# Final norm of an encoder block: load the residual before the last two expert blocks are added, and redo their rows afterwards

## What is computed

```python
x = x + _hier_moe(_rmsnorm(x, norm_ffn_g), ...)   # each token: 2 of 32 experts
return _rmsnorm(x, norm_final_g)

# in _hier_moe: the (token, expert) pairs are sorted by expert, each expert's list is
# padded to whole blocks of 128 rows, and each block gives
a = silu(xblk @ w1[e]) * (xblk @ w3[e])
yb = a @ w2[e]                                     # scaled by the gate, added to the token's row
```

## Time and profile before

| | us |
|---|---|
| median of 3 runs | 2211.6 |
| lowest, highest | 2208.79, 2212.04 |
| profiled execution, device time | 2216.69 |
| its span in the trace | 2214.9 |
| mean granted TensorE clock | 0.952 of full |

### The profile page before, as it was taken

The page is one execution under the profiler, slowest core; times in us unless marked ns, Lnnn a source line. Parts: engine busy times, 40 slices in busy tenths (PEclk is TensorE's granted clock), DMA queues, the critical chain, the costliest instruction groups (busy, mean ns, idle before and its releaser), DMA issues. The chain is left out here.

```text
span 2214.9 us, 29378 instructions
## 1 busy us (share of the span) xinstructions
PE 1995.7 (90%) x8823; PEld 1404.3 (63%) x8824; DVE 1212.4 (55%) x1133; ACT 1063.1 (48%) x1283; POOL 817.7 (37%) x526
## 2 busy tenths in 40 slices
PE   3999999999999977979999389999898999999980
PEld 2436778777666322327777268888686888888870
DVE  6653223234667734744444655566767666665644
ACT  6871222226556332433333244555757556555634
POOL 0690000000000320322222055576867866675750
PEclk9999999999999998989999679999999999999995
DMA  6691222321234987957443358788989987887848
GB/s 218 238 327 39 76 67 76 95 76 41 50 79 137 348 310 301 347 196 238 169 152 105 143 171 277 218 307 291 370 287 371 376 286 249 306 291 224 304 132 322
DMA packets 206334, 476.88 MB, mean 215 GB/s; under 512 B 23569, under 2 KB 86165, under 8 KB 201111
## 3 DMA queue, kind: packets, MB, share of 16 engines
q1 hardware_dynamic: 165080, 383.61, 47.3%
q0 software_dynamic: 17824, 58.79, 11.6%
q10 hardware_dynamic: 23360, 33.56, 4.8%
HBM read 355.25 MB, written 114.29 MB: 212 GB/s over the span
## 5 line engine op out<-in xcount | busy, mean ns | idle before, releaser
L1921 PE MATMUL p<-wh_hi,x_hi 128*128 128x512 f32 x768 | 313.2, 408 | 22.2 <-DVE wh_lo L2048 14.2
L1867 POOL DMA_INDIRECT xg<-scratch_H,curidx x196 | 285.3, 1456 | 89.8 <-issue 44.8
L1921 PE MATMUL p<-wh_lo,x_hi 128*128 128x512 f32 x768 | 307.7, 401 | 0.0
L1921 PE MATMUL p<-wh_hi,x_lo 128*128 128x512 f32 x768 | 307.4, 400 | 0.0
L2048 DVE TENSOR_TENSOR wh_lo<-w_raw,wh_hi 128x2048 fp32r<-128x2048 f32 x128 | 284.7, 2285 | 26.1 <-ACT wh_hi L1996 26.1
L540 PE MATMUL ps<-h_hi,wp_hi 128*128 128x512 f32 x640 | 257.6, 403 | 4.3 <-DVE wp_lo L735 4.3
L540 PE MATMUL ps<-h_lo,wp_hi 128*128 128x512 f32 x640 | 254.3, 397 | 0.0
L540 PE MATMUL ps<-h_hi,wp_lo 128*128 128x512 f32 x640 | 254.3, 397 | 0.0
L1996 ACT ACTIVATE wh_hi<-w_raw 128x2048 fp32r<-128x2048 f32 x128 | 234.0, 1903 | 0.0
L1886 POOL TENSOR_TENSOR wy_lo<-w_raw,wy_hi 128x2048 fp32r<-128x2048 f32 x32 | 187.7, 5865 | 90.8 <-ACT wy_hi L1999 90.5
L1921 PEld LDWEIGHTS p<-wh_hi,x_hi 128*128 128x128 f32 x768 | 147.0, 191 | 59.1 <-DVE wh_lo L2048 15.8
(11 more groups left out here) (329 smaller groups left out, 3588.8 us busy)
## 6 DMA issues: line engine op xcount, KB each, us to landing
w_raw<-in_exp_w_dram SPq DMA_DIRECT2D x384, 512.0 KB, 7.5
dec<-in_decay_dram SPq DMA_DIRECT2D x32, 512.0 KB, 5.5
scratch_KA<-work SPq DMA_DIRECT2D x32, 512.0 KB, 4.5
scratch_SI<-arena SPq DMA_DIRECT2D x32, 512.0 KB, 4.5
kin<-scratch_KA SPq DMA_DIRECT2D x21, 512.0 KB, 7.5
arena<-scratch_SA SPq DMA_DIRECT2D x21, 512.0 KB, 6.0
wp_raw<-in_w_in_dram SPq DMA_DIRECT2D x18, 512.0 KB, 3.8
h_raw<-in_x_dram ACTq DMA_DIRECT2D x4, 2048.0 KB, 15.3
```

The costliest lines, as they stand in the source:

```text
L1867: pool.indirect_dma_start(out=xg[:, j, :], out_offset=None, in_=quarter_rows, in_offset=bass.IndirectOffsetOnAxis(ap=cur[:, j:j + 1], axis ...
L1921: mm = pe.matmul(acc[:, :], x[:, k, :], w, start=(k == 0 and i == 0), stop=(k == n - 1 and i == 2))
```

## The change

Four things change. (1) POOL no longer adds the two last blocks before it lets SP start: it raises `mostly_added` when the loop's last scatter has landed and PE has used the last first-layer weights. (2) `final_norm` treats all 16 tiles as before. POOL waits for the 16 loads, then scatters the two last results one after the other, gathers the rows of these two blocks (128 each) from `X2`, waits for all 32 stores, and scatters the two normed tiles over `out`, waiting for the first before it issues the second. ACT and DVE norm them as tiles 16 and 17. The row lists come from `spot`: `late_row` is `spot` cut at 2047, so every empty row becomes row 2047, and `late_out` its place in `out`. Four small DVE operations in `route` make them. (3) The second late result has a buffer of its own, `yb_last`, and ACT stores it when it has come to tile 5. (4) For the last expert, the sixth weight split moves from POOL to DVE.

The core of the diff:

```diff
 # route, vector
+            dve.wait_ge(idx_set, BASE + 2)
+            step(dve.tensor_scalar(late_row[:, :], spot[:, :], SEQ - 1, None, ALU.min))
+            step(dve.tensor_scalar(late_out[:, :], late_row[:, :], HALF - 1, 5, ALU.bitwise_and, ALU.logical_shift_left))
+            step(dve.tensor_scalar(late_tile[:, :], late_row[:, :], 6, None, ALU.arith_shift_right))
+            dve.tensor_tensor(late_out[:, :], late_out[:, :], late_tile[:, :], ALU.add).then_inc(weight_set, 1)
 # experts, gpsimd
             def split_last(e, B, r):
+                if e is LAST:
+                    return
...
             B = per_block(pool, "pool", body, split_last)
-            for last in range(2):
-                scatter(B + last)
-                added(B + last)
-            pool.sem_inc(all_added, 1)
+            pool.wait_ge(used, BASE + B * KC)
+            pool.sem_inc(mostly_added, 1)
             pool.wait_ge(xg_in, B * 64 + 128)
             pool.sem_inc(pool_passed, 1)
+            pool.wait_ge(marks["weight_set"], BASE + 2)
+            for last in range(2):
+                for i, rows_of in enumerate((late_row, late_out, spot)):
+                    pool.tensor_copy(cur_late[:, last, i:i + 1], rows_of[:, ds(B + last, 1)]).then_inc(late_ready, 1)
+            for t in range(NT):
+                pool.wait_ge(marks["x_in"][t], 16)
+            pool.wait_ge(late_ready, BASE + 6)
+            for last, y in enumerate((yb, yb_last)):
+                pool.wait_ge(y_evac, BASE + B + last + 1)
...
+                pool.indirect_dma_start(out=rows, out_offset=bass.IndirectOffsetOnAxis(ap=cur_late[:, last, 2:3], axis=0),
+                                        in_=y[:, :], in_offset=None, compute_op=ALU.add).then_inc(y_out, 16)
+                pool.wait_ge(y_out, B * 16 + 16 * last + 16)
...
+            for last in range(2):
+                pool.indirect_dma_start(out=marks["x_late"][:, last, :], out_offset=None, in_=token_rows,
+                                        in_offset=bass.IndirectOffsetOnAxis(ap=cur_late[:, last, 0:1], axis=0)).then_inc(late_in[last], 16)
+            pool.wait_ge(marks["o_out"], 32 * NT)
+            for last in range(2):
+                pool.wait_ge(marks["late_normed"], last + 1)
+                pool.indirect_dma_start(out=dram["out"].rearrange("o t d -> (o t) d"), out_offset=bass.IndirectOffsetOnAxis(ap=cur_late[:, last, 1:2], axis=0),
+                                        in_=marks["x_late"][:, last, :], in_offset=None).then_inc(late_stored, 16)
+                pool.wait_ge(late_stored, 16 * last + 16)
 # experts, scalar
-            for last in range(2):
-                store_y(B + last)
-            act.sem_inc(act_passed, 1)
+            store_y(B)
+            marks["store_last"] = lambda: store_y(B + 1, yb_last)
 # experts, vector
             def split_w(e, B, r, some=range(D_PAIRS)):
-                for pair in some:
+                for pair in (range(PAIRS) if e is LAST else some):
 # final_norm, sync
-            sp.wait_ge(marks["all_added"], 1)
+            sp.wait_ge(marks["mostly_added"], 1)
 # final_norm, scalar
-            for t in range(NT):
-                if t + 1 < NT:
+            for t in range(NT + 2):
+                if t == STORE:
+                    marks["store_last"]()
+                if t + 1 < NT + 2 and t + 1 != NT:
                     square(t + 1)
                 act.wait_ge(inverse, t + 1)
                 act.activation(st[:, t, 3:4], st[:, t, 2:3], ACT.Sqrt).then_inc(root, 1)
+                if t + 1 == NT:
+                    square(NT)
 # final_norm, vector
-            for t in range(NT):
-                if t + 1 < NT:
+            for t in range(NT + 2):
+                if t + 1 < NT + 2 and t + 1 != NT:
                     invert(t + 1)
                 dve.wait_ge(root, t + 1)
...
+                dve.scalar_tensor_tensor(out=tile(t), in0=tile(t), scalar=st[:, t, 3:4], in1=gain[:, :],
+                                         op0=ALU.mult, op1=ALU.mult).then_inc(o_ready if t < NT else late_normed, 1)
```

More of the change, by code:

```diff
@@ L1582, in route @@
         marks.update(idx_set=idx_set, weight_mm=weight_mm, weight_set=weight_set)
-        LG, weight, idx, spot, nblk, tables = yield sem
+        LG, weight, idx, spot, nblk, tables, late_row, late_out = yield sem
         cursor = dict(wy=marks["wy_at"], xg=marks["xg_at"])
@@ L1610, in route @@
         ex, one1 = sb("ex", [P, NT]), sb("one1", [P, NT])
+        late_tile = put("wy", "late_tile", [P, IDX_COLS], I32)
         assert cursor["wy"] <= marks["wy_end"] and cursor["xg"] <= marks["xg_end"]
@@ L1771, in experts @@
         pool_passed, act_passed = sem("pool_passed"), sem("act_passed")
-        xg_in, y_out, all_added = sem("xg_in", 0), sem("ye_out", 0), sem("all_added", 0)
-        marks["all_added"] = all_added
+        xg_in, y_out, mostly_added = sem("xg_in", 0), sem("ye_out", 0), sem("mostly_added", 0)
+        marks["mostly_added"] = mostly_added
         rounded, lowered, lowered_last, used = sem("w_rnd"), sem("w_low"), sem("w_low_last"), sem("w_used")
-        D_PAIRS = PAIRS - 1
+        D_PAIRS, LAST = PAIRS - 1, N_EXP - 1
         spot_ready, y_added = sem("spot_ready"), sem("y_added")
+        late_ready, late_in, late_stored = sem("late_ready"), [sem(f"late_in{i}", 0) for i in range(2)], sem("late_stored", 0)
+        marks["late_in"] = late_in
         idx_ready, trx, xhi_ready, xlo_ready = sem("idx_ready"), sem("trx"), sem("xhi_ready"), sem("xlo_ready")
@@ L1779, in experts @@
             sem(n) for n in ("s_ready", "a_ready", "tra", "ahi_ready", "alo_ready", "y_done", "y_evac"))
-        nblk, idx, spot, weight, xT = yield sem
+        nblk, idx, spot, weight, xT, late_row, late_out = yield sem
         marks["raw_at"] = -(-nc.sbuf_base // 32) * 32
@@ L1790, in experts @@
         cur, cur_spot = sb("curidx", [P, 4], I32), sb("curspot", [P, 1], I32)
+        cur_late = sb("curlate", [P, 2, 3], I32)
         marks["xg_at"] = nc.sbuf_base
         xg = sb("xg", [P, 4, D // 4])
+        x_hi_at = -(-nc.sbuf_base // 32) * 32
         x_hi, x_lo = sb("x_hi", [P, KC, P], F32R), sb("x_lo", [P, KC, P], F32R)
@@ L1825, in per_block @@
                 blocks_of(N_EXP - 2, 0)
-                following(N_EXP - 1, eng.snap(B), 1)
+                following(LAST, eng.snap(B), 1)
                 blocks_of(N_EXP - 1, 1)
@@ L1978, in split_a, with store_y @@
                 act.activation(a_hi[:, :, :], pta.rearrange("p (k n) -> p k n", k=FT), ACT.Copy).then_inc(ahi_ready, 1)
-            def store_y(B):
+            def store_y(B, out=yb):
                 act.wait_ge(y_done, BASE + B + 1)
-                act.wait_ge(y_added, BASE + B)
+                if out is yb:
+                    act.wait_ge(y_added, BASE + B)
+                else:
+                    act.wait_ge(xlo_ready, BASE + B * 2)
                 for c in range(2):
-                    copy = act.activation(yb[:, c * 512:(c + 1) * 512], py[c][:, :], ACT.Copy, scale=weight[:, ds(B, 1)])
+                    copy = act.activation(out[:, c * 512:(c + 1) * 512], py[c][:, :], ACT.Copy, scale=weight[:, ds(B, 1)])
                 copy.then_inc(y_evac, 1)
@@ L2004, in _ @@
             split_w(0, 0, 0, range(H_PAIRS, PAIRS))
-            act.wait_ge(marks["weight_set"], BASE + 1)
+            act.wait_ge(marks["weight_set"], BASE + 2)
             act.wait_ge(a_ready, BASE + 1)
@@ L2050, in split_w @@
                         hi, lo = (v[:, r * FT + j - KC:r * FT + j - KC + 2, :] for v in wy)
-                        dve.tensor_tensor(lo, raw[:, j:j + 2, :], hi.bitcast(F32), ALU.subtract).then_inc(lowered, 1)
+                        dve.tensor_tensor(lo, raw[:, j:j + 2, :], hi.bitcast(F32), ALU.subtract).then_inc(lowered if pair < D_PAIRS else lowered_last, 1)
             dve.memset(a[:, :], 0.0).then_inc(a_ready, 1)
@@ L2078, in final_norm @@
         x_in = [sem(f"x8_in{t}", 0) for t in range(NT)]
-        squared, mean, inverse, root, o_ready = (sem(n, 0) for n in ("f_squared", "f_mean", "f_inverse", "f_root", "f_out"))
+        squared, mean, inverse, root, o_ready, late_normed = (sem(n, 0) for n in ("f_squared", "f_mean", "f_inverse", "f_root", "f_out", "late_normed"))
+        marks.update(x_in=x_in, o_out=o_out, late_normed=late_normed)
         yield sem
@@ L2082, in final_norm @@
         x, junk = at("xfin", [P, NT, D], marks["wh_at"]), at("junk8", [P, 2, D], marks["raw_at"])
-        gain, st = at("gain_fin", [P, D], marks["raw_at"] + 8 * D), at("st8", [P, NT, 4], marks["raw_at"] + 12 * D)
+        gain, st = at("gain_fin", [P, D], marks["raw_at"] + 8 * D), at("st8", [P, NT + 2, 4], marks["raw_at"] + 12 * D)
+        marks["x_late"] = x_late = at("x_late", [P, 2, D], marks["raw_at"] + 16 * D)
+        tile = lambda t: x[:, t, :] if t < NT else x_late[:, t - NT, :]
         out_t = dram["out"].rearrange("o (n l g) d -> l g n (o d)", g=2, l=NT)
+        STORE = 5
         block = yield
@@ L2102, in square @@
```

(23 more changed lines are left out.)

5 lines of the change are left out of this document (4 added, 1 removed).

## The result

| | before | changed |
|---|---|---|
| median of 5 runs, us | 2211.6 | 2221.6 |
| lowest, highest | 2208.79, 2215.10 | 2218.57, 2225.51 |
| ratio, 95% interval | | 1.0047, 1.0030 to 1.0065 |
| profiled execution, us (span) | 2216.69 (2214.9) | 2220.03 (2218.3) |

The change makes the kernel 10 us slower, 6.6 to 14.4. I had forecast no change (+0.6), with 2204 to 2229 as the range and 0.38 for slower.

A forecast was written before the change was run, and what follows sets the result against it. The tail was taken as bound by waits, then by saturated transfers after the first load. Start -23.6, loads +0.5 and work behind the last load +23.7 gave net +0.6, 2212.2 us on the median; 8-in-10 range 2204 to 2229.

The forecast's parts named there:

- 4, gathers: Two gathers of 4 KB rows after the late adding scatters: last landing 7.0 us after its start, ends 3.2 and 9.
- last landing to end: Close of the span: 0.4 us from the last landing to the end, as in the kernel before.
- one-for-one rule: Tail: whatever moves the first load moves the end equally, so long as nothing is put behind the stores.
- Part 1: Start of the tail: earlier release of SP and the moved weight split bring the first load 23.6 us earlier, to 2145.5.
- Part 3: Two late adding scatters, serial beside stores: 9.2 us each, 0.9 before each start, 0.5 for the port shared with VectorE.
- Part 6: Wait for the 32 stores: they end at 2200.3, 3.4 us ahead of the normed tile 16, so it costs nothing.
- Part 7: Two serial scatters over `out` behind everything: 4.8 us each plus 0.9 before each, 0.5 of each for empty rows.
- writes to one row: Rival, scatters over `out`: 129 empty rows write row 2047 singly at 0.158 us, +15.9 us, 2228.1; chance 0.15.
- Part 8: Small things: four DVE list operations in `route`, about 1 us, covered by DVE's idle wait; POOL's index copies also covered.
- crowded queue: Rival: late scatters, port, second gather, release and scatters over `out` all at their upper ends, +8.5 us, 2220.7; chance 0.20.
- light queue: Rival: late scatters take 6.2 us and gathers 4.2, so the stores gate, 2207.0 on the median; chance 0.20.
- likeliest case: The forecast itself: net +0.6 us, 2212.2 on the median, between 2207.8 and 2216.6; chance 0.42.

The follow-up runs named there:

- before_pool_last: The kernel before with one wait more: POOL waits for the 32 stores as its last act; 2212.22 us against 2210.22, ratio 1.0007.
- after_no_late: The changed kernel without its late scatters, gathers and scatters over `out`, so it ends with the 32 stores; 2194.00 us against 2210.22 for before, ratio 0.9929.
- after_pool_split: The changed kernel with the last expert's sixth weight split back on POOL; 2223.81 us against 2209.61 for before, ratio 1.0060.

## Why the prediction was right or wrong, step by step

Times are counted from the start of ACT's `yb` in the loop's last pass, so that both kernels have one clock.

| step of the prediction | forecast | measured | difference |
|---|---|---|---|
| 1, `yb` to first load | 9.6 | 11.6 | +2.0 |
| 2, to last load landed | 25.2 | 26.1 | +0.9 |
| 3, first scatter, with its start | 10.6 | 13.5 | +2.9 |
| 3, second scatter, with its start | 10.1 | 10.2 | +0.1 |
| 4, gathers | 9.2 | 8.0 | -1.2 |
| 5, norm | 3.1 | 2.8 | -0.3 |
| 7, two scatters over `out` | 11.4 | 8.0 | -3.4 |
| last landing to end | 0.4 | 4.65 | +4.25 |
| sum | 79.6 | 84.8 | +5.2 |

**The step that failed** is the last one, "+ 0.4": the tail of SP was taken for that of POOL. before_pool_last shows it by itself, with 3.8 of the 4.25. That the rows above it sum to only +1.0 is luck: +5.9 in the first four against -4.9 in the next three. The one-for-one rule ("whatever moves the first load moves the end") held, 21.0 in after_no_late.

**Part 1** was right in mechanism and 2.0 too early: the scatter's copy was held by DVE's two splits. That the sequencer runs ahead of the fourth gather was right: SP starts at 2145.11, the fourth gather at 2145.26.

**Part 3** named the right cause and undersized the first scatter: 12.4 and 12.1 beside a full backlog of stores, where beside weight loads 9.9 was the most of 50. The second, with the backlog running out, was sized right in this profile (9.3 against 9.2) and came to 10.0 and 11.2 in two others. The 0.5 for the port was not needed.

**Part 6** held: the stores were done at 2194.7 + 3.8 = 2198.5, 7 ahead of the first normed late tile, and 65.0 after `yb` where the forecast's 2200.3 makes 64.4.

**Part 7** was oversized: 3.6 and 3.3 for 512 KB, nearer to the 3.2 of the Trainium skill's formula ("DMA: Bandwidth & Descriptors", "Anatomy of one DMA — SWDGE (gpsimd) path") than to my 4.8. The trace agrees with the page for a plain scatter on a quiet DMA. The first, with 87 empty rows on row 2047, took 0.3 more than the second with 42. At 0.158 a write the 45 writes between them would make 7.1, so the rival of writes to one row is dead.

**Part 8**, "small things", held the rest of the loss. The lists cost nothing that can be told, as argued; that a 24-byte tile shifts everything behind it in SBUF was not in the sum at all, and it costs 5.1 (2.9 to 7.5).

**The rivals.** The crowded queue was half right: first scatter beyond its bound, but not the gathers nor the last scatters. The light queue did not come. The change did what it says. The likeliest case was wrong in size: tail +5.8 to +6.7 and shift +5 make 11 to 12, where the runs show 10 to 11 and I had +0.6. That 2221.6 lies in my range, and within 1 us of the crowded queue's 2220.7, is luck: the range was made wide for landings, while POOL's drain and the shift, some 9 us together, stand in no rival. Even with neither POOL's drain nor the shift, the change would have been worth about nothing: what it gains at the start of the loads (21.0) it spends behind them (26.8, of which the drain is 4.25).

## What to carry to other kernels

Work that is taken off the front of a transfer-bound tail and redone behind it must be priced as a serial chain, landing by landing, under the load that the moved transfers themselves make; here two adding scatters, two gathers and two scatters, with POOL's drain behind them, cost 27 us for 21 gained. Look at which engine ends last before and after a change and at its closing drain: under the line that ends the block, POOL's takes 3.8 to 4.2 us, DVE's 2.1, SP's nothing. And when the profiles' affected stretch explains only part of a timed loss, build the kernel with the change's allocations alone: a tile that nothing uses cost 5 us here, nearly as much as the tail had lost.

## What the runs showed of the hardware beyond what I expected

- POOL's DRAIN at the end of a block took 3.82 to 4.15 us, whether POOL had just issued a transfer or none for 50 us, and 5.37 when it began while its last scatter was still landing.
- Plain indirect scatters of 512 KB landed 3.3 and 3.6 after their start on a quiet DMA; adding ones 6.1 and 6.2 quiet, 9.3 to 13.0 beside stores.
- Stores of 256 KB from 64 partitions, with no load beside them, moved 418 GB/s while a backlog stood (landing 8 to 11 us after issue) and 275 without one (landing 4.0 after issue). From two issuing engines they moved 336 and then 251 behind the loads.
- A POOL copy of 128 values took 2.34 us beside VectorE's subtractions, 0.65 right behind a subtraction of POOL's own (after_pool_split), and 0.18 elsewhere in the tail.
- A shift of the tiles behind a 24-byte allocation made a 2210 us kernel 5 us slower, with the same instructions.
